# A two-layer hybrid decoder trunk on one core: the second half of layer 0's Q and K by token halves, with four query tiles of the first head between

## The chip, the cores and the metric

One core of a Trainium2 chip runs the whole program. The metric is the time of one execution in device microseconds. TensorE (PE) multiplies, VectorE (DVE), ScalarE (ACT) and GpSimd (POOL) do the rest, SyncE (SP) issues the transfers.

## The reference

Input and output are 1024 tokens x 1024 channels, float32. Layer 0 has differential attention (four heads, two 64-wide maps each) beside a pooling mixer, layer 1 a gated short convolution beside dilated attention with three branches; both end in an output projection and a SwiGLU block. What the change touches:

```python
q, k, v, u = jnp.split(proj, [qk_w, 2 * qk_w, 2 * qk_w + A_WIDTH], axis=-1)
q = rmsnorm(q.reshape(bsz, seq, 2, A_HEADS, HEAD_DIM), ev_q_gain[i])
k = rmsnorm(k.reshape(bsz, seq, 2, A_HEADS, HEAD_DIM), ev_k_gain[i])
...
s = jnp.einsum('bqmhd,bkmhd->bmhqk', qb, k, preferred_element_type=jnp.float32) * scale
s = s - slopes[:, None, None] * dist.astype(jnp.float32)
p = jax.nn.softmax(jnp.where(dist >= 0, s, -jnp.inf), axis=-1)
a = p[:, 0] - lam * p[:, 1]
o = jnp.einsum('bhqk,bkhd->bqhd', a.astype(v.dtype), v)
...
ya = (rmsnorm(ya, ev_subln_gain[i]) * (1.0 - lambda_init)).reshape(bsz, seq, A_WIDTH)
```

## The kernel before

**Split products.** Every float32 operand of a large product is split into a high part, made by ScalarE (`copy`, L1671), and a low part, the difference, made by VectorE (`low`, L2220) or GpSimd. A product is three matmuls of 512 columns (`mm3`, L1142 to L1144): high x high, low x high, high x low.

**Q and K.** The Q and K columns of layer 0 come in two halves `s`. A half runs over four quarters `q` of the channels; for each, SP loads raw weights (RQ, L661 on), ScalarE and VectorE split them into the buffers WQh and WQl (number r = 4s + q, two buffers by turns), and TensorE adds six matmuls to each of eight banks, one for each tile of 128 tokens. In the last quarter each bank ends with `qk_pe`. Then, for each token tile, ScalarE squares (SQ), VectorE sums (QSS, L2480) and scales (QMS, L2481), GpSimd raises to the power -1/2 (QRS, L1009, in a loop), VectorE applies it (QN, L2496), TensorE turns it by four transposes (`qk_turn`, L1352) and ScalarE writes it out (QK). In the first quarter of the second half TensorE also does two mixings (`mix`) of the pooling mixer.

**Attention of layer 0.** It runs over four heads, here units, of eight query tiles each, 32 tiles n. For a tile: scores of two maps (`score`, L1196 and L1197: keys K against queries QST, or K1X, K2X, QX in unit 0); bias and row extreme (`biased`, L2524: PR, NMX); exponential with its sum (`expo`, L1881); VectorE's reciprocal, ratio and combined tile (`combine`, L2578, semaphore `c_ok`); TensorE's transposes (`turn`, L1226); ScalarE's copy PT (`turned`); the product with V (`weigh`, L1238); ScalarE's squared sum and scaled copy (`scaled`, L1969: YJ, then Y). The order on every engine is written out by hand, and semaphores carry the rest. TensorE scores tile n+2, weighs n-1 and turns n. The stage begins when Q and K are all done.

**The keys of the next unit.** The keys and queries of unit u+1 are split while unit u runs: `next_stack` on ScalarE, `low_stacks` on GpSimd (K, L1019, and QST), each behind a combined tile (`behind_sum` waits for `c_ok`). When both K low parts exist, SP issues four transfers (L701, L702) that copy K with its halves of the partitions swapped (`staged`), and the first score of the next unit waits for all four. From tile n=7 on TensorE fills its time with blocks of the output projection (`out_block`, weights QWh and QWl, whose low part GpSimd makes at L1035).

**Layer 1** has the same loop over tiles with three branches; its ScalarE splits the next unit's keys in `following`, behind i=1 and i=2.

```python
def behind_sum(n):
    pool.wait_ge(c_ok, n + 1)
```

## Time and profile before

| | us |
|---|---|
| median of 3 runs | 2162.61 |
| fastest and slowest | 2161.91, 2162.73 |
| the profiled execution | 2162.4 |
| its span in the profile | 2160.5 |
| TensorE busy | 2126.2 (98%) |
| VectorE busy | 1306.7 (60%) |
| ScalarE busy | 900.1 (42%) |
| GpSimd busy | 862.0 (40%) |

The profiled execution's own time is 1.9 us longer than its span, which begins with the first and ends with the last instruction. The granted clock of TensorE is 0.9 or more of full speed in all 40 slices. In the views below a row gives the start, the duration, the engine, the line, the operation and the tiles; in brackets stand the idle time before it and what ended it.

### The profile page before, as it was taken

The page shows a single profiled execution, that of the slowest core. Times are in us where ns is not written, and L with a number is a line of the kernel's source. Part 1 is how long each engine was busy: PE and PEld are TensorE (multiplying, and loading weights), DVE is VectorE, ACT ScalarE, POOL GpSimd, SP SyncE. Part 2 cuts the span into 40 slices and gives each one's busy share as a digit, 9 for nine tenths or more (in the row PEclk, how much of TensorE's full clock was granted, in tenths as well). Part 3 has the DMA queues.
Part 4 walks back from the last instruction along what each step waited for, and adds up shares of the span by engine and source line. Part 5 has one row for each costly group of instructions (what it writes and reads, how often), then busy time and mean ns, then how long its engine had stood idle before and what let it go on. Part 6 is the DMA issues. An engine that isn't in the chain of part 4 may idle for free.

```text
span 2160.5 us, 30068 instructions
## 1 busy us (share of the span) xinstructions
PE 2126.2 (98%) x10572; PEld 1773.0 (82%) x10572; DVE 1306.7 (60%) x1725; ACT 900.1 (42%) x1497; POOL 862.0 (40%) x571
## 2 busy tenths in 40 slices
PE   8999899999999999999999999999999999999999
PEld 7877799888888888888888887888888888888887
DVE  4344775775565565558597347765865556555555
ACT  4134875443333333445333137853433333334432
POOL 1022432456677663002064024320577667751000
PEclk9999999999999999999999999999999999999999
DMA  5012321055554557676302120411265554558665
GB/s 193 0 52 56 127 79 30 20 168 202 187 185 164 175 175 261 198 244 194 117 20 59 59 69 21 135 44 38 69 205 190 198 174 153 169 176 283 194 194 195
DMA packets 229534, 295.55 MB, mean 137 GB/s; under 512 B 11824, under 2 KB 133168, under 8 KB 229168
## 3 DMA queue, kind: packets, MB, share of 16 engines
q1 hardware_dynamic: 229136, 294.04, 41.8%
q8 instruction: 68, 1.11, 0.2%
q14 instruction: 42, 0.34, 0.1%
q10 hardware_dynamic: 288, 0.05, 0.0%
HBM read 208.06 MB, written 77.59 MB: 132 GB/s over the span
## 4 chain that ended last, share of the span: by engine, by line
PE 80%; issue 13%; ACT 4%; POOL 2%; DVE 2%; DMA 1%; POOLq 0%; SPq 0%; ACTq 0%; DVEq 0%
PE PS L1613 12%; PE PS L1614 12%; PE PS L1615 12%; PE PS L1640 6%; PE PS L1642 6%; PE PS L1641 6%; PE PS L1142 4%; PE PS L1144 4%; PE PS L1143 4%; PE PS L1226 2%; PE PS L1265 1%; POOL QRS L1009 1%; ACT PR L1881 1%; PE PS L1331 1%; PE PS L1332 1%
## 5 line engine op out<-in xcount | busy, mean ns | idle before, releaser
L2220 DVE TENSOR_TENSOR LINEl<-LINE,HIGH 128x1024 fp32r<-128x1024 f32 x154 | 194.6, 1273 | 163.6 <-ACT HIGH L1671 163.5
L1671 ACT ACTIVATE HIGH<-LINE 128x1024 fp32r<-128x1024 f32 x154 | 162.7, 1060 | 232.2 <-PE PS L1642 208.2
L1640 PE MATMUL PS<-HIGH 128*128 128x512 f32 x616 | 240.2, 390 | 0.4 <-DVE LINEl L2220 0.4
L1642 PE MATMUL PS<-HIGH,LINEl 128*128 128x512 f32 x616 | 239.7, 389 | 0.0
L1641 PE MATMUL PS<-LINEl,HIGH 128*128 128x512 f32 x616 | 239.7, 389 | 0.0
L2220 DVE TENSOR_TENSOR SLOTl<-BLOCKS,RING 128x512 fp32r<-128x512 f32 x168 | 154.4, 919 | 95.6 <-ACT RING L1671 90.8
L941 POOL TENSOR_TENSOR ST<-ST 128x512 f32<-128x512 f32 x132 | 191.9, 1454 | 32.7 <-DMA ST<-in_ffn_w_down 24.1
L1671 ACT ACTIVATE RING<-BLOCKS 128x512 fp32r<-128x512 f32 x168 | 105.9, 630 | 227.8 <-PE PS L1615 221.5
L2220 DVE TENSOR_TENSOR SLOTl<-SLOT,RING 128x512 fp32r<-128x512 f32 x126 | 131.8, 1046 | 86.6 <-ACT RING L1671 86.3
L1009 POOL TENSOR_TENSOR QRS<-QMS,EXPO 128x8 f32<-128x8 f32 x32 | 52.1, 1638 | 220.7 <-DVE QMS L2481 220.1
L1640 PEld LDWEIGHTS PS<-HIGH 128*128 128x128 f32 x616 | 115.6, 188 | 24.9 <-DVE LINEl L2220 1.1
L1642 PEld LDWEIGHTS PS<-HIGH,LINEl 128*128 128x128 f32 x616 | 115.6, 188 | 24.0
L1641 PEld LDWEIGHTS PS<-LINEl,HIGH 128*128 128x128 f32 x616 | 115.7, 188 | 23.9
L1671 ACT ACTIVATE RING<-SLOT 128x512 fp32r<-128x512 f32 x126 | 79.2, 630 | 125.3 <-PE PS L1615 115.0
L1613 PE MATMUL PS<-B1h,RING 128*128 128x512 f32 x336 | 130.7, 389 | 0.0
L1614 PE MATMUL PS<-B1l,RING 128*128 128x512 f32 x336 | 130.7, 389 | 0.0
L1615 PE MATMUL PS<-B1h,SLOTl 128*128 128x512 f32 x336 | 130.7, 389 | 0.0
L913 POOL TENSOR_TENSOR SLOT<-BLOCKS 128x512 f32<-128x512 f32 x42 | 55.2, 1314 | 189.0 <-DMA BLOCKS<-in_ffn_w_up 189.0
L946 POOL TENSOR_TENSOR RST<-MSQ,EXPO 128x1 f32<-128x1 f32 x32 | 22.8, 714 | 224.3 <-DVE MSQ L2238 224.3
L1142 PE MATMUL PS<-WQh,HH 128*128 128x512 f32 x256 | 102.5, 400 | 0.6 <-DVE U L2533 0.6
L1144 PE MATMUL PS<-WQh,HL 128*128 128x512 f32 x256 | 99.9, 390 | 0.0
L1143 PE MATMUL PS<-WQl,HH 128*128 128x512 f32 x256 | 99.7, 389 | 0.0
(426 smaller groups left out, 5703.8 us busy)
## 6 DMA issues: line engine op xcount, KB each, us to landing
LINE<-hidden SPq DMA_DIRECT2D x154, 256.0 KB, 2.8
hidden<-HID SPq DMA_DIRECT2D x44, 512.0 KB, 4.3
ST<-in_ffn_w_down SPq DMA_DIRECT2D x44, 512.0 KB, 4.1
sums<-ST SPq DMA_DIRECT2D x22, 1024.0 KB, 6.1
hidden<-ST SPq DMA_DIRECT2D x22, 1024.0 KB, 6.7
LINE<-sums SPq DMA_DIRECT2D x88, 256.0 KB, 3.0
BLOCKS<-in_ffn_w_gate SPq DMA_DIRECT2D x42, 512.0 KB, 4.0
BLOCKS<-in_ffn_w_up SPq DMA_DIRECT2D x42, 512.0 KB, 5.2
```

Of the source, the lines that this page charges most:

```text
L941: nc.gpsimd.tensor_tensor(dst, x, y, op).then_inc(st_sum, 1)
L1142: pe.matmul(dst, lh, rh, start=first, stop=False)
L1143: pe.matmul(dst, lh, rl, start=False, stop=False)
L1144: return pe.matmul(dst, ll, rh, start=False, stop=last)
L1613: pe.matmul(dst, lh, rh[:, k, :], start=k == 0 and not adds_on, stop=False, skip_group_check=adds_on)
L1614: pe.matmul(dst, lh, rl[:, k, :], start=False, stop=False, skip_group_check=adds_on)
L1615: last = pe.matmul(dst, ll, rh[:, k, :], start=False, stop=k == 3, skip_group_check=adds_on)
L1640: pe.matmul(dst, hi[:, 0, ts], hi[:, 1, :], start=j == 0 and not adds_on, stop=False, skip_group_check=adds_on)
L1641: pe.matmul(dst, hi[:, 0, ts], lo[:, 1, :], start=False, stop=False, skip_group_check=adds_on)
L1642: pe.matmul(dst, lo[:, 0, ts], hi[:, 1, :], start=False, stop=j == NJ - 1, skip_group_check=adds_on).then_inc(dn_pe, 1)
L1671: return nc.scalar.activation(dst, src, ACT.Copy, **kw)
L2220: return v.tensor_tensor(dst, src, hi.bitcast(F32), ALU.subtract)
```

## The change

The second half of layer 0's Q and K is done by token halves: four quarters for token tiles 0 to 3, then four for tiles 4 to 7, in the order 2, 3, 1, 0, so that two of the weight buffers are kept and two (r=8, 9) are loaded and split again. Between the matmuls of the second token half stand the QK turns of tiles 0 to 3, the scores of tiles n=0 to 4 and the turns and weighings of n=0 to 3 of unit 0, with banks of their own (`score_at`, `turn_bank`, `weighed`) and outputs in a tile Y0. ScalarE's and VectorE's orders follow. The squared sum writes into the tile of the scaled copy, which now waits for it (`y_sq`). GpSimd's powers are unrolled; the low part of the first output weights is done in four rows of 256 columns between the last powers, and all low parts of unit 1's keys and first queries stand behind the combined tile n=4 (they stood behind n=2, 3 and 4). SP issues the tables before the loads of r=6 on, and the swap of unit 0 ahead of the output weights. In layer 1 ScalarE's high parts of the next keys stand behind i=0 and within i=1 (they stood behind i=1 and i=2), and two high parts of the convolution's columns move likewise in the last unit.

The core of the diff:

```diff
+        WQ_AT = (0, 10)
+        EARLY = 4
+        def score_at(L, m, n):
+            return 512 * m if L == 0 and n < EARLY else 1024 * m
+        def y_at(n):
+            return Y0[:, n, :] if n < EARLY else Y[:, n % NT, P * (n // NT):P * (n // NT) + P]
...
+                for r in range(6):
+                    load_qk(r, r // 4, r % 4)
+                if L == 0:
+                    load_tables()
+                    for r, q in ((6, 2), (7, 3), (8, 1), (9, 0)):
+                        load_qk(r, 1, q)
+                    swap_keys(0)
+                    sp.wait_ge(wq_lo, WQ_AT[1])
+                    load_quarter(0)
...
+                def low_quarter_row(k):
+                    if k == 0:
+                        pool.wait_ge(wo_hi, SPLIT_AT["q0"])
+                    ins = nc.gpsimd.tensor_tensor(QWl[0][:, k, :], QWs[0][:, k, :], QWh0[:, k, :].bitcast(F32), ALU.subtract)
+                    if k < 3:
+                        ins.then_inc(pool_part, 1)
+                        pool.wait_ge(pool_part, k + 1)
+                    else:
+                        ins.then_inc(wo_lo, 1)
+                        pool.wait_ge(wo_lo, SPLIT_AT["q0"])
...
-                    low_w("q0", QWl[0][:], QWs[0][:], QWh0[:])
-                    behind_sum(2)
-                    low_stacks(1, 0)
-                    behind_sum(3)
-                    low_stacks(1, 1)
-                    behind_sum(4)
-                    low_stacks(1, 2, 3)
+                    qk_power(2 * NT - 4)
+                    qk_power(2 * NT - 3)
+                    pool.wait_ge(qk_rs, 2 * NT - 2)
+                    low_quarter_row(0)
+                    qk_power(2 * NT - 2)
+                    pool.wait_ge(qk_rs, 2 * NT - 1)
+                    low_quarter_row(1)
+                    qk_power(2 * NT - 1)
+                    pool.wait_ge(qk_rs, 2 * NT)
+                    low_quarter_row(2)
+                    low_quarter_row(3)
+                    behind_sum(EARLY)
+                    low_stacks(1, 0, 1, 2, 3)
...
+                def qk_group(t, q, step):
+                    ts = slice(P * t, P * t + P)
+                    for r in range(2):
+                        last = mm3(bank(t), HH[:, 2 * q + r, ts], HL[:, 2 * q + r, ts], WQh[q % 2 if step < 6 else 1 - q % 2][:, r, :],
+                                   WQl[q % 2 if step < 6 else 1 - q % 2][:, r, :], step % 4 == 0 and r == 0, step % 4 == 3 and r == 1)
+                    if step % 4 == 3:
+                        last.then_inc(qk_pe, 1)
+                    elif step in (0, 1, 4, 5) and t % 4 == 3:
+                        last.then_inc(wq_pe[0], 1)
+                def qk_by_tokens():
+                    for step in range(4):
+                        pe.wait_ge(wq_lo, 4 + step + 1)
+                        for t in range(4):
+                            if step == 0:
+                                pe.wait_ge(bank_free[0], NT + t + 1)
+                                pe.wait_ge(mix_ok, 2)
+                            qk_group(t, step, step)
+                            if step == 0 and t < 2:
+                                mix(2 + t)
+                    pe.wait_ge(mix_ok, 4)
+                    for step, q in ((4, 2), (5, 3), (6, 1), (7, 0)):
+                        if step >= 6:
+                            pe.wait_ge(wq_lo, step + 3)
+                        for t in range(4, NT):
+                            if step == 4:
+                                pe.wait_ge(bank_free[0], NT + t + 1)
+                            qk_group(t, q, step)
+                            k = 4 * (step - 4) + t - 4
+                            if k < 4:
+                                qk_turn(1, k)
+                            if k == 3:
+                                pe.wait_ge(staged[0], 64)
+                                pe.wait_ge(stack_lo, 4)
+                                pe.wait_ge(bank_free[0], 2 * NT + 2)
+                                both_scores(0)
+                            elif k == 4:
+                                both_scores(1)
+                            elif k == 6:
+                                both_scores(2)
+                                turn(0, 0, 0, 0)
+                            elif k == 7:
+                                weigh(0)
+                            elif k == 8:
+                                both_scores(3)
+                                turn(0, 0, 0, 1)
+                            elif k == 9:
+                                weigh(1)
+                            elif k == 10:
+                                turn(0, 0, 0, 2)
+                            elif k == 11:
+                                weigh(2)
+                                turn(0, 0, 0, 3)
+                            elif k == 12:
+                                weigh(3)
+                                pe.wait_ge(s_mx[1][0], EARLY + 1)
+                                score(0, 0, 0, 0, EARLY)
+                            elif k == 14:
+                                pe.wait_ge(t_ea[0][0], EARLY)
+                                pe.wait_ge(o_ok[0], EARLY + 2)
+                                score(0, 1, 0, 0, EARLY)
+                    qk_turn(1, 4)
+                    qk_turn(1, 5)
+                    both_scores(5)
+                    qk_turn(1, 6)
+                    turn(0, 0, 0, EARLY)
+                    qk_turn(1, 7)
+                    both_scores(6)
...
+                def scaled(n):
+                    u, i = n // NT, n % NT
+                    c = 2 * (i % 4)
+                    act.wait_ge(o_pe[0], n + 1)
+                    nc.scalar.activation(y_at(n), weighed(n), ACT.Square, scale=RDN[:, c:c + 1],
+                                         accum_out=YSS[:, n:n + 1]).then_inc(y_sq, 1)
+                    act.wait_ge(y_sq, n + 1)
+                    copy(y_at(n), weighed(n), scale=RDN[:, c:c + 1]).then_inc(o_ok[0], 1)
...
-                    nc.scalar.activation(YJ[:], weighed(n), ACT.Square, scale=RDN[:, c:c + 1],
-                                         accum_out=YSS[:, n:n + 1]).then_inc(y_sq, 1)
-                    copy(Y[:, i, P * u:P * u + P], weighed(n), scale=RDN[:, c:c + 1]).then_inc(o_ok[0], 1)
...
+                    qk_square(1, 0)
+                    qk_square(1, 1)
+                    qk_square(1, 2)
+                    qk_out(1, 0)
+                    qk_square(1, 3)
+                    qk_out(1, 1)
+                    qk_out(1, 2)
+                    split_qk(0, 8)
+                    qk_out(1, 3)
+                    expos(0)
+                    expos(1)
+                    turned(0, 0, 0)
+                    expos(2)
+                    split_qk(0, 9)
+                    scaled(0)
+                    turned(0, 0, 1)
+                    expos(3)
+                    scaled(1)
+                    turned(0, 0, 2)
+                    scaled(2)
+                    turned(0, 0, 3)
+                    qk_square(1, 4)
+                    scaled(3)
+                    qk_square(1, 5)
+                    qk_square(1, 6)
+                    high_w("q0", QWh0[:], QWs[0][:])
+                    qk_out(1, 4)
+                    qk_square(1, 7)
+                    expos(EARLY)
+                    qk_out(1, 5)
+                    next_stack(0, 1, 1, 0, 1)
+                    qk_out(1, 6)
+                    expos(EARLY + 1)
+                    turned(0, 0, EARLY)
+                    qk_out(1, 7)
+                    next_stack(0, 1, 1, 2, 3)
+                    high_u(2, stacks_before(0, 1) + 2)
+                    for n in range(EARLY + 1, TILES0):
...
+                        if i == 1:
+                            following(1)
+                        if n == TILES0 - 7:
+                            channel_high(1)
                         turned(1, g, i)
                         if n + 1 < TILES0:
                             expo(1, g, i + 1)
-                        following(*{1: (0,), 2: (1,), 3: (2, 3), 4: (4,), 5: (5,)}.get(i, ()))
+                        following(*{0: (0,), 3: (2, 3), 4: (4,), 5: (5,)}.get(i, ()))
...
+                    qk_stats(1, 0)
+                    qk_stats(1, 1)
+                    qk_apply(1, 0)
+                    qk_stats(1, 2)
+                    qk_apply(1, 1)
+                    qk_stats(1, 3)
+                    qk_apply(1, 2)
+                    qk_apply(1, 3)
+                    biased(0, 0, 0, 0)
+                    biased(1, 0, 0, 0)
+                    split_qk(0, 8)
+                    for n in range(EARLY):
+                        if n + 1 < EARLY:
+                            if n > 0:
+                                dve.wait_ge(c_ok, n)
+                            biased(0, 0, 0, n + 1)
+                        for m in range(2):
+                            dve.wait_ge(s_ex[m][0], n + 1)
+                        denominators(n)
+                        if n + 1 < EARLY:
+                            biased(1, 0, 0, n + 1)
+                        ratio(n)
+                        combine(n)
+                        if n == 1:
+                            split_qk(0, 9)
+                    qk_stats(1, 4)
+                    dve.wait_ge(c_ok, EARLY)
+                    biased(0, 0, 0, EARLY)
+                    qk_stats(1, 5)
+                    qk_apply(1, 4)
+                    biased(1, 0, 0, EARLY)
+                    qk_stats(1, 6)
+                    qk_apply(1, 5)
+                    qk_stats(1, 7)
+                    qk_apply(1, 6)
+                    for n in range(EARLY, TILES0):
```

How the rows move, at three places. First TensorE, where the second half of Q and K ends and unit 0 begins (IDN is the identity of a transpose, QN a normalised QK tile, K1X and K2X the keys of unit 0 and their swapped copy, QX its queries). Before:

```order
L1352 MATMUL PS<-IDN,QN_102 128x128 [waits qk_n]
L1352 MATMUL PS<-IDN,QN_102 128x128 x3
L1196 MATMUL PS<-K1X_339,QX_343 128x256 [waits s_mxA0]
L1197 MATMUL PS<-K2X_341,QX_343 128x256
L1196 MATMUL PS<-K1X_340,QX_344 128x256 [waits s_mxB0]
L1197 MATMUL PS<-K2X_342,QX_344 128x256
L1352 MATMUL PS<-IDN,QN_103 128x128 [waits qk_n]
L1352 MATMUL PS<-IDN,QN_103 128x128 x3
L1196 MATMUL PS<-K1X_339,QX_343 128x384 [waits s_mxA0,stack_lo,mix_ok]
L1197 MATMUL PS<-K2X_341,QX_343 128x384
L1196 MATMUL PS<-K1X_340,QX_344 128x384 [waits s_mxB0]
L1197 MATMUL PS<-K2X_342,QX_344 128x384
```

And in the changed kernel, in the middle of the second token half, where PR are combined tiles and PT their turned copies:

```order
L1276 MATMUL PS<-IDN,PR_353 128x128 [waits c_ok,t_eaA0]
L1276 MATMUL PS<-IDN,PR_353 128x128 x2
L1189 MATMUL PS<-WQh_54,HH 128x512
L1190 MATMUL PS<-WQl_56,HH 128x512
L1191 MATMUL PS<-WQh_54,HL 128x512
L1189 MATMUL PS<-WQh_54,HH 128x512
L1190 MATMUL PS<-WQl_56,HH 128x512
L1191 MATMUL PS<-WQh_54,HL 128x512
L1288 MATMUL PS<-V,PT_349 128x128 [waits o_ok0,t_eaA0]
L1288 MATMUL PS<-V,PT_349 128x128 x2
L1276 MATMUL PS<-IDN,PR_354 128x128 [waits c_ok,t_eaA0]
L1276 MATMUL PS<-IDN,PR_354 128x128 x3
```

Turns and weighings of unit 0 stand between groups of QK matmuls, where before unit 0's scores came only behind the last of them.

Second, GpSimd from the last powers to UL. Before:

```order
L1009 TENSOR_TENSOR QRS<-QMS,EXPO 128x8 [waits qk_ms]
L1006 REGISTER_ALU
L1006 COMPARE_AND_BRANCH
L1035 TENSOR_TENSOR QWl_81<-QWs_77,QWh_85 128x1024 [waits wo_hi]
L1019 TENSOR_TENSOR K_333<-QK,K_333 64x1024 [waits stack_hi,stack_lo,c_ok,wo_lo]
L1019 TENSOR_TENSOR K_334<-QK,K_334 64x1024 [waits stack_hi,stack_lo,c_ok]
L1019 TENSOR_TENSOR QST_104<-QK,QST_104 64x256 [waits stack_hi,stack_lo,c_ok]
L1019 TENSOR_TENSOR QST_105<-QK,QST_105 64x256 [waits stack_lo,stack_hi]
L1030 TENSOR_TENSOR UL_70<-U,UH_66 128x1024 [waits uh_hi,c_ok,stack_lo]
```

In the changed kernel:

```order
L1048 TENSOR_TENSOR QWl_81<-QWs_77,QWh_85 128x256 [waits wo_hi,qk_rs]
L1035 TENSOR_TENSOR QRS<-QMS,EXPO 128x8 [waits qk_ms,pool_part]
L1048 TENSOR_TENSOR QWl_81<-QWs_77,QWh_85 128x256 [waits qk_rs]
L1035 TENSOR_TENSOR QRS<-QMS,EXPO 128x8 [waits qk_ms,pool_part]
L1048 TENSOR_TENSOR QWl_81<-QWs_77,QWh_85 128x256 [waits qk_rs]
L1048 TENSOR_TENSOR QWl_81<-QWs_77,QWh_85 128x256 [waits pool_part]
L1060 TENSOR_TENSOR K_333<-QK,K_333 64x1024 [waits stack_hi,stack_lo,c_ok,wo_lo]
L1060 TENSOR_TENSOR K_334<-QK,K_334 64x1024 [waits stack_lo,stack_hi]
L1060 TENSOR_TENSOR QST_104<-QK,QST_104 64x256 [waits stack_lo,stack_hi]
L1060 TENSOR_TENSOR QST_105<-QK,QST_105 64x256 [waits stack_lo,stack_hi]
L1071 TENSOR_TENSOR UL_70<-U,UH_66 128x1024 [waits uh_hi,c_ok,stack_lo]
```

QWl is made in four pieces, and the second K waits for no combined tile of its own; the first still does, for a later one.

Third, ScalarE in the second and third tile of a unit of layer 1. Before:

```order
L1671 ACTIVATE PT_350<-PS 128x128 [waits o_pe1,t_peB1]
L1881 ACTIVATE PR_354,DEN<-PR_354,NMX 128x256 [waits s_mxB1]
L1671 ACTIVATE PTB_355<-PS 128x256 [waits o_pe1,t_peA1]
L1881 ACTIVATE PR_351,DEN<-PR_351,NMX 128x384 [waits s_mxA1]
L1671 ACTIVATE PTB_356<-PS 128x256 [waits o_pe1,t_peB1]
L1881 ACTIVATE PR_353,DEN<-PR_353,NMX 128x384 [waits s_mxB1]
L1671 ACTIVATE K_333<-QK 64x1024
L1671 ACTIVATE PT_349<-PS 128x384 [waits o_pe1,t_peA1]
L1881 ACTIVATE PR_352,DEN<-PR_352,NMX 128x512 [waits s_mxA1]
L1671 ACTIVATE PT_350<-PS 128x384 [waits o_pe1,t_peB1]
L1881 ACTIVATE PR_354,DEN<-PR_354,NMX 128x512 [waits s_mxB1]
L1671 ACTIVATE K_334<-QK 64x1024
```

In the changed kernel:

```order
L1999 ACTIVATE PR_352,DEN<-PR_352,NMX 128x256 [waits s_mxA1]
L1789 ACTIVATE PT_350<-PS 128x128 [waits o_pe1,t_peB1]
L1999 ACTIVATE PR_354,DEN<-PR_354,NMX 128x256 [waits s_mxB1]
L1789 ACTIVATE K_333<-QK 64x1024
L1789 ACTIVATE PTB_355<-PS 128x256 [waits o_pe1,t_peA1]
L1999 ACTIVATE PR_351,DEN<-PR_351,NMX 128x384 [waits s_mxA1]
L1789 ACTIVATE K_334<-QK 64x1024
L1789 ACTIVATE PTB_356<-PS 128x256 [waits o_pe1,t_peB1]
L1999 ACTIVATE PR_353,DEN<-PR_353,NMX 128x384 [waits s_mxB1]
L1789 ACTIVATE PT_349<-PS 128x384 [waits o_pe1,t_peA1]
L1999 ACTIVATE PR_352,DEN<-PR_352,NMX 128x512 [waits s_mxA1]
```

Both K high parts now stand ahead of the exponential of 128x384 of the second map, and the first of them ahead of the first map's.

## Rows read from the trace of the kernel before

**Rows 1.** The page, busy time of TensorE.

```profile
PE 2126.2 (98%) x10572; PEld 1773.0 (82%) x10572; DVE 1306.7 (60%) x1725; ACT 900.1 (42%) x1497; POOL 862.0 (40%) x571
```

**Rows 2.** TensorE's waits, 212 to 246: waited for, us, times, longest.

```profile
PE PS L1238 <- ACT PT L1671: 4.9, 5, 1.7
PE PS L1352 <- DVE QN L2496: 1.6, 2, 1.1
PE PS L1196 <- DVE NMX L2524: 1.2, 3, 0.7
```

**Rows 3.** Timeline of TensorE around the first score of unit 1.

```profile
236.04 0.30 PE L1196 MATMUL PS<-K,QST 128*128 128x128 f32 x1
...
237.40 1.60 PE L1238 MATMUL PS<-V,PT 128*128 128x128 f32 x12 [0.94 <-ACT PT L1671]
...
242.07 1.83 PE L1238 MATMUL PS<-V,PT 128*128 128x128 f32 x14 [1.69 <-ACT PT L1671]
...
244.77 0.36 PE L1142 MATMUL PS<-QWh,UH 128*128 128x256 f32 x1
```

**Rows 4.** Timeline of TensorE in the second half of Q and K.

```profile
195.18 0.39 PE L1142 MATMUL PS<-WQh,HH 128*128 128x512 f32 x1
...
203.79 0.39 PE L1144 MATMUL PS<-WQh,HL 128*128 128x512 f32 x1
```

**Rows 5.** ScalarE's groups by form, 160 to 300: busy, mean ns, idle.

```profile
L1913 ACT ACTIVATE SQ<-PS 128x512 f32<-128x512 f32 x8 | 4.8, 597 | 15.6 <-PE PS L1144 15.6
```

**Rows 6.** VectorE's groups by form, 160 to 300.

```profile
L2496 DVE TENSOR_TENSOR QN<-PS,QRS 128x256 f32<-128x256 f32 x18 | 6.8, 420 | 1.4 <-POOL QRS L1009 1.2
...
L2480 DVE TENSOR_REDUCE QSS<-SQ 128x8 f32<-128x512 f32 x8 | 5.4, 680 | 11.0 <-ACT SQ L1913 11.0
...
L2220 DVE TENSOR_TENSOR WQl<-RQ,WQh 128x1024 fp32r<-128x1024 f32 x3 | 3.7, 1224 | 7.9 <-ACT WQh L1671 7.8
...
L2578 DVE SCALAR_TENSOR_TENSOR PR<-PR,SCB,PR 128x640 f32<-128x640 f32 x3 | 2.6, 880 | 0.0
...
L2524 DVE CUSTOM_DVE_ANT_0 PR<-PS,BX 128x768 f32<-128x768 f32 x2 | 1.9, 958 | 0.0
```

**Rows 7.** Timeline of GpSimd, 199 to 246.

```profile
201.74 13.29 POOL L1009 TENSOR_TENSOR QRS<-QMS,EXPO 128x8 f32<-128x8 f32 x8 [41.91 <-DVE QMS L2481]
215.00 2.39 POOL L1035 TENSOR_TENSOR QWl<-QWs,QWh 128x1024 fp32r<-128x1024 f32 x1
...
226.02 2.41 POOL L1019 TENSOR_TENSOR K<-QK,K 64x1024 fp32r<-64x1024 f32 x1 [0.69 <-DVE PR L2578]
```

**Rows 8.** Timeline of SyncE's issues, 228 to 231.

```profile
228.45 0.46 SPq L701 DMA_DIRECT2D K<-K  x1
...
230.25 1.12 SPq L702 DMA_DIRECT2D K<-K  x1
```

**Rows 9.** Issue to landing: transfers one and three (L701), then the fourth (L702).

```profile
DMA to landing us min/median/max: 3.0/3.7/4.4
...
DMA to landing us min/median/max: 4.8/4.8/4.8
```

**Rows 10.** Timeline of ScalarE, one scaled tile of unit 0.

```profile
221.98 0.19 ACT L1969 ACTIVATION_READ_ACCUMULATOR YJ<-PS,RDN 128x1 f32 x1
222.07 0.35 ACT L1671 ACTIVATE Y<-PS,RDN 128x128 f32<-128x128 f32 x1
```

**Rows 11.** TensorE's waits, 245 to 420.

```profile
PE PS L1238 <- ACT Y L1671: 0.8, 4, 0.3
```

**Rows 12.** Timeline of ScalarE in unit 1 of layer 1.

```profile
1349.32 1.06 ACT L1671 ACTIVATE K<-QK 64x1024 fp32r<-64x1024 f32 x1
```

**Rows 13.** Timeline of TensorE in the same unit.

```profile
1345.16 0.55 PE L1226 MATMUL PS<-IDN,PR 128*128 128x128 f32 x3
...
1352.00 0.77 PE L1226 MATMUL PS<-IDN,PR 128*128 128x128 f32 x5 [0.99 <-ACT PR L1881]
```

**Rows 14.** Timeline of VectorE, combined tile n=0.

```profile
216.79 0.74 DVE L2578 SCALAR_TENSOR_TENSOR PR<-PR,SCB,PR 128x128 f32<-128x128 f32 x1
```

358 lines of the change are left out of this document (193 added, 165 removed).

## The prediction

> **What bounds the kernel now.** I read the page first: TensorE is busy for 2126.2 of the span's 2160.5 us [rows 1], its granted clock is full in every slice, and the chain that ended last is four fifths TensorE's. The number of its matmuls does not change, so the time can only come out of its idle gaps. The profiled execution took 2162.4 us, 0.2 below the median of 2162.61; the sum goes against its span and carries over unchanged. A measurement tells about 0.2%, 4.3 us, from no change.
>
> The next view is TensorE's waits in the stretch the change rebuilds. Between 212 and 246 us it waits 7.7 us for three things: 4.9 for ScalarE's copy of the turned tile (PT), 1.6 for VectorE's normalised Q and K (QN) and 1.2 for VectorE's row extremes (NMX) [rows 2]. With a start-up of some tenths behind each of the ten, that is the most this part can win, 8 to 10 us. The reader should see that these gaps stand in two places, ahead of the first score of unit 1 (tile n=8, at 236.04) and behind it, 0.94 and 1.69 [rows 3]. From that score on TensorE's list of work is the same before and after, and what it has done up to it is the same too, in another order. So the question is when that score can start.
>
> **1. The earlier steps.** A step of the second half is 48 matmuls long now; from 195.18 to 203.79 there are 38 intervals, 0.2266 each [rows 4], so a step is 10.9 us and a half step 5.4. The half steps need split weights twice as often. For the fourth half step (r=7), buffer 1 is free when the second ends, about 176.6 (a start at 162.3, 10.9 for two half steps, 3.4 for the two mixings); ScalarE's high part takes 1.06, as the keys' of 1024 columns [rows 12], and VectorE's low part 1.22 [rows 6], so 178.9 if neither is busy and about 180.5 behind a UL and a hand-over. It is needed at 182.0. I cost it at nothing: the mixings and the third half step hide it. If that cover were gone, every us of lateness over 1.5 is one at the end. The two extra splits (r=8, 9) add 2.1 to ScalarE, 2.4 to VectorE and four loads to SP; their half steps come 11 us behind their buffers' release, so the four score and turn groups between them hide these, at nothing. In units of work ScalarE has room: eight squares at 0.60 [rows 5], the outputs, eight exponentials and four scaled tiles come to some 23 us of 31.
>
> **2. When the K swap of unit 1 can start.** SP issues it once GpSimd's two low parts of the keys are made. Before, the second ran from 226.02 for 2.41 [rows 7], the first of four transfers was issued at 228.45 and the last at 230.25 [rows 8], which took 4.8 to land [rows 9]: 6.6 from first issue to last landing, 235.0. The score came at 236.04 without a wait.
>
> After, both low parts stand behind the combined tile n=4. I follow that back. Tile 5's last matmul group ends at 162.3 + 30 groups x 1.36 + 3.4 for mixings + 1.8 for four turned QK tiles + about 6.8 for unit 0's pieces put in between = 215.1. Then its square 0.60, its sums 0.68 [rows 5, 6], a scaling of about 0.2, and GpSimd's power 1.66 (eight took 13.29 [rows 7]): 218.3. GpSimd now puts a quarter of the low part of the output weights, 2.39 for 1024 columns [rows 7] and so about 0.7 for 256, between powers, and the power for tile 6 ends at 220.8. VectorE applies it in 0.8 (two of 0.42), makes the row extremes of two tiles of 768 keys, 0.96 each, one small ratio and the combined 128x640 of 0.88 [rows 6]: 224.8. Two low parts make it 229.8, and the swap lands at 229.8 + 6.6 = 236.4. TensorE, which without any wait would be at that score near 228 (236.04, less 5.1 for the waits ahead of it, less about 0.3 of start-up behind each), waits for it. It waits on the way too, for QN of tiles 5 and 6 (about 1.4), for the combined tile n=4 (about 2.5) and for row extremes (about 1), and would be there at 233. None of that is summed: the swap, 3.5 us later, decides. **Term 1: +0.4 to +0.6, I take +0.5.** Bounds: if TensorE did not wait for the swap, 233 against 236.04, -3.0, and -3.5 with a shorter wait on the way; if the low parts ran 1 us later, +1.5.
>
> **3. Behind that score.** While TensorE waits, ScalarE and VectorE get ahead. Of 0.94 and 1.69 [rows 3] I leave 1.0 and 0.3. **Term 2: -1.3** (0 to -2.6). The first fill, at 244.77 before [rows 3], would come near 244.0.
>
> **4. The scaled tiles.** Square and scaled copy now write the same tile, so the copy waits for the square's accumulator. In the trace the copy starts at 222.07, 0.10 before the accumulator read ends (221.98 + 0.19) [rows 10]; with the wait it starts about 0.05 behind that end, so each tile costs ScalarE 0.15. The Trainium skill's page "ScalarE: Activation LUTs", section "What ACT_TABLE_LOAD costs", says that ACTIVATEs back to back overlap by about 93 ns; by that alone a tile would lose 0.09 and this term would be 0.7 instead of 1.2. The row's overlap of 0.10 agrees with it, and the hand-over is what I add. 24 tiles follow in units 1 to 3, 3.6 us in all, but TensorE waits for ScalarE's copy (Y) only in four of them, 0.8 us [rows 11]; the rest is hidden under the output blocks. I let a third reach the path. **Term 3: +1.2** (0 to +3.6).
>
> **5. Layer 1.** The keys' second high part, at 1349.32, delays the exponential behind it, for which TensorE's five turns wait 0.99 until 1352.00 [rows 12, 13]. Moved between the exponential of i=2 and the turned copy, and the first one an iteration earlier, 1.05 us now stands before the exponential for the three turns at 1345.16, which have no wait and no slack now [rows 13]. One wait of about 1.0 goes and one comes, in each of four units. **Term 4: +0.1** (-1 to +2). Late next, had the first high part been free, would be the QST copies.
>
> Sum: 0.5 - 1.3 + 1.2 + 0.1 = **+0.5 us, 2163.1**. The early work fills TensorE's gaps, but it then stands before the same swap.
>
> **The rivals.**
>
> *The gain is kept* (faster). The swap is not waited for so long, since GpSimd's low parts or the transfers end sooner. For it: the powers leave a loop and may be shorter, and the transfer share is low before the swap. Against it: each low part ran 2.39 and the four landings are spread by SP's own issue, 1.12 for the last [rows 8]. If the fourth transfer landed 3.0 after its issue, as the first did [rows 9], the swap took 4.8 and not 6.6; if the power and the low parts also came 1 us sooner, the score starts 2.8 earlier: 2160.3. In the bound, with no wait there at all, term 1 is -3.5 and the end 2159.1; with term 3 at nothing 2157.9. The page "DMA: Bandwidth & Descriptors" of the Trainium skill, section "Latency and other measured facts", gives about 600 ns to a first byte on such a queue; the row with 4.8 for a transfer of an undisturbed swap speaks against taking that as the whole price.
>
> *The turned copies are late at the early tiles* (slower). Four weighings now stand between QK groups, and TensorE's order is fixed: each waits for ScalarE's PT behind squares, splits and exponentials, as the five later ones do at 4.9/5 = 0.98 each [rows 2]. It decides from about 0.5 us of lateness, which is the room I find at them. Priced at 0.98 x 4 = 3.9, with the end of QK, and so the swap, later by that: 2163.1 + 3.9 = 2167.0. For it: VectorE may be held up beside GpSimd, since a combined tile of 128 keys took 0.74 while GpSimd's QWl ran, against 0.88 for 640 keys [rows 6, 14]. Against it: ScalarE's 23 of 31 us, and GpSimd is idle through the early tiles.
>
> *The moves do nothing*: gaps only change places in both layers, the self-wait is hidden: 2162.6. This and my forecast cannot be told apart by the time alone.
>
> **How the numbers follow.** The forecast with the nothing case: 0.76. The gain kept: 0.16, of which 0.08 goes beyond 4.3 us (under 2158.3). Turned copies late: 0.08, of which 0.06 beyond. Faster 0.09, same 0.84, slower 0.07. The range takes in the faster rival's middle and, above, the ends of terms 1 and 3 together: 2159.0 to 2166.0.
>
> **What would show it.** In the changed trace: no wait of TensorE between 163 and 218; waits at the fifth and sixth QK turns, then a longer one for the combined tile n=4 near 225; the wait for unit 1's keys of about 4 us ending near 236.5, and the swap's first issue near 229.9; fill near 244; more waits for Y in the main loop than 0.8; in layer 1 waits of about 1.0 at the three turns, none at the five. It is wrong if that wait for the keys is under 2 us, if waits stand among the QK groups, or if the layer 1 waits do not mirror each other.

## The result and the profile after

| | before | changed |
|---|---|---|
| median of 20 runs each, same chip | 2162.70 | 2165.97 |
| fastest and slowest | 2161.91, 2164.38 | 2163.90, 2169.03 |
| the profiled execution | 2162.4 | 2165.93 |
| its span | 2160.5 | 2164.1 |

The ratio is 1.0015, 95% interval 1.0008 to 1.0021: 3.3 us longer, inside the 0.2% (4.3 us) that the prediction calls no change, but with an interval that leaves 1 out. The forecast was 2163.1 with a range of 2159.0 to 2166.0, so the median lies inside the range, at its upper edge. The sum said +0.5 and the measurement says +3.3; most of what follows is about that difference.

The page of the changed kernel: its span, busy times, granted clock and chain (compare [rows 1]).

```profile
span 2164.1 us, 29989 instructions
...
PE 2128.2 (98%) x10572; PEld 1776.2 (82%) x10572; DVE 1302.6 (60%) x1728; ACT 906.2 (42%) x1499; POOL 871.3 (40%) x574
...
PEclk9999999999999999999999999999999999999999
...
PE 92%; ACT 3%; DVE 2%; POOL 1%; issue 1%; DMA 1%; SPq 0%; ACTq 0%; DVEq 0%; POOLq 0%
```

The page hides what matters here: TensorE is busy for 2.0 us more than before with the same work, and the row of clocks still shows only nines. TensorE's waits of the changed kernel from 160 to 246 us (waited for, us, times, longest), the counterpart of [rows 2]:

```profile
PE PS L1276 <- issue: 2.5, 1, 2.5
PE PS L1244 <- DMA K<-K: 2.2, 1, 2.2
PE PS L1244 <- DVE NMX L2693: 1.3, 2, 0.8
PE PS L1402 <- DVE QN L2665: 1.0, 1, 1.0
PE PS L1288 <- ACT PT L1789: 0.8, 1, 0.8
PE PS L1189 <- DVE U L2755: 0.6, 1, 0.6
```

The 4.9 us for PT have become 0.8. In their place stand 2.5 ahead of the turn of the combined tile n=4 (listed as "issue"; VectorE's combination of that tile ends at 225.32 and the turn starts at 225.41) and 2.2 for unit 1's keys. The last row is the one at 162, from which the rebuilt stretch begins; between it and 218 there is none. TensorE's timeline around the two standing waits, and to the first fill (L1189):

```profile
225.41 1.30 PE L1276 MATMUL PS<-IDN,PR 128*128 128x128 f32 x5 [2.53 <-issue]
...
237.49 0.33 PE L1244 MATMUL PS<-K,QST 128*128 128x128 f32 x1 [2.22 <-DMA K<-K]
...
237.76 2.33 PE L1288 MATMUL PS<-V,PT 128*128 128x128 f32 x12
...
242.92 1.83 PE L1288 MATMUL PS<-V,PT 128*128 128x128 f32 x14 [0.78 <-ACT PT L1789]
...
245.62 0.36 PE L1189 MATMUL PS<-QWh,UH 128*128 128x256 f32 x1
```

The first score of unit 1 starts 1.45 later than before and the fill, at 245.62, is 0.85 later than the 244.77 of [rows 3]. The wait for keys was there, and one wait of 0.78 in place of 0.94 and 1.69. But the 12 weighings at 237.76 took 2.33, where before they took 1.60 [rows 3]. What GpSimd, SyncE and VectorE did ahead of the swap (one fence for each):

```profile
223.90 2.00 POOL L1048 TENSOR_TENSOR QWl<-QWs,QWh 128x256 fp32r<-128x256 f32 x2
225.98 4.90 POOL L1060 TENSOR_TENSOR K<-QK,K 64x1024 fp32r<-64x1024 f32 x2
```

```profile
230.90 0.46 SPq L699 DMA_DIRECT2D K<-K  x1
...
232.69 1.12 SPq L700 DMA_DIRECT2D K<-K  x1
```

```profile
224.21 1.11 DVE L2712 SCALAR_TENSOR_TENSOR PR<-PR,SCB,PR 128x640 f32<-128x640 f32 x1
...
229.86 2.10 DVE L2677 SCALAR_TENSOR_TENSOR BIAS<-DIST,SM,MASK 128x1024 f32<-128x1024 f32 x1
```

The combined tile ends at 225.32, the low parts at 230.88, the swap is issued at 230.90 and TensorE goes on 6.59 later: the chain that the prediction followed, each link 0.5 to 1.0 late. GpSimd's last two rows of output weights, at 223.90, end only at 225.90 and then the keys begin.

The granted clock of TensorE shows where its longer busy time comes from. Stretches of the changed kernel (PE busy, PEld, DVE, ACT, POOL, then the granted clock, DMA share and GB/s):

```profile
222.00:224.00 2.00, 0.88 (x7) 0.47 (x5) 2.00 (x7) 1.98 (x6) 1.84 (x3) 1.00 0.00 0
224.00:225.00 1.00, 0.00 (x0) 0.00 (x0) 0.96 (x2) 0.97 (x2) 0.92 (x2) 0.84 0.00 0
225.00:228.00 3.00, 2.59 (x11) 2.52 (x12) 0.98 (x3) 3.00 (x7) 2.92 (x2) 0.50 0.00 0
...
236.00:238.00 2.00, 0.51 (x4) 0.51 (x5) 1.97 (x4) 1.97 (x7) 0.77 (x1) 1.00 0.38 59
238.00:239.00 1.00, 1.00 (x8) 1.00 (x8) 0.42 (x3) 1.00 (x2) 0.74 (x1) 0.67 0.73 238
239.00:241.00 2.00, 2.00 (x12) 2.00 (x11) 0.17 (x1) 0.96 (x3) 1.07 (x1) 0.50 1.04 406
241.00:242.00 1.00, 1.00 (x7) 0.94 (x5) 0.00 (x0) 0.05 (x1) 0.00 (x0) 0.62 0.76 274
```

Twice, once behind each standing wait, the granted clock is 0.50: 1.2 GHz of the 2.4. The first time its cost is swallowed by the wait for the keys. The second time little is waited for (0.8 for PT), and everything up to the fill pays. A third fall lies at the very start: the mean clock from 10 to 20 us is 0.83 in this profile and in those of kernels 1, 3, 4, 7, 9 and 10 below, and 1.00 in the others and before. Here it cost nothing that can be seen, since the rebuilt stretch begins at 162.16, and at 162.33 before.

Behind the fill, TensorE's waits for the scaled tiles from 245 to 420 us, against 0.8 in four [rows 11]; its waits for the exponentials in layer 1 from 1300 to 1440, where before had 5.6 us in nine with a longest of 1.2; and its timeline there, at the three turns that had no wait in [rows 13]:

```profile
PE PS L1288 <- ACT Y L1789: 2.4, 8, 0.5
```

```profile
PE PS L1276 <- ACT PR L1999: 5.4, 9, 0.9
```

```profile
1348.71 0.55 PE L1276 MATMUL PS<-IDN,PR 128*128 128x128 f32 x3 [0.90 <-ACT PR L1999]
```

The account of the profiled execution by these rows: +0.85 at the fill, +1.6 in the waits for Y, and +3.6 in the span, so about 1.1 is left. It stands in layer 1, in three small waits of TensorE: 1.3 for X where before had 0.5, 2.2 for QN where before had 1.9, and 0.5 for PTB where before had 0.2, less the 0.2 that the exponentials gave back.

```profile
PE PS L1189 <- DVE X L2578: 1.3, 1, 1.3
```

### The profile page after: what moved, and what is told of

It reads as the page before. It is cut to its first block, busy times and chain, and to the rows that moved or that the text cites. A ratio compares the mean times of both kernels' runs of the same rounds, so it can differ in the third digit from the quotient of the medians.

```text
span 2164.1 us, 29989 instructions
## 1 busy us (share of the span) xinstructions
PE 2128.2 (98%) x10572; PEld 1776.2 (82%) x10572; DVE 1302.6 (60%) x1728; ACT 906.2 (42%) x1499; POOL 871.3 (40%) x574
## 3 DMA queue, kind: packets, MB, share of 16 engines
q8 instruction: 68, 1.11, 0.2%
## 4 chain that ended last, share of the span: by engine, by line
PE 92%; ACT 3%; DVE 2%; POOL 1%; issue 1%; DMA 1%; SPq 0%; ACTq 0%; DVEq 0%; POOLq 0%
PE PS L1733 12%; PE PS L1731 12%; PE PS L1732 12%; PE PS L1189 7%; PE PS L1191 7%; PE PS L1190 7%; PE PS L1758 6%; PE PS L1760 6%; PE PS L1759 6%; PE PS L1276 2%; PE PS L1315 2%; PE PS L1381 1%; PE PS L1380 1%; PE PS L1382 1%; PE PS L1288 1%; PE PS L1207 1%
## 5 line engine op out<-in xcount | busy, mean ns | idle before, releaser
L972 POOL TENSOR_TENSOR RST<-MSQ,EXPO 128x1 f32<-128x1 f32 x32 | 22.8, 714 | 224.8 <-DVE MSQ L2407 224.8
L1189 PE MATMUL PS<-WQh,HH 128*128 128x512 f32 x256 | 103.2, 403 | 0.6 <-DVE U L2755 0.6
```

Source lines behind the costliest of these rows:

```text
L1189: pe.matmul(dst, lh, rh, start=first, stop=False)
```

## The experiments

Three sets of four kernels ran, each set on one chip beside the kernel before (33 runs of it a set, 11 of each other kernel). The interval of a ratio is about 2 us to either side throughout, so a profile's rows carry more than a median does. The profiles do not all reach the rebuilt stretch at the same time: its first matmul starts between 162.00 and 163.15 us (162.33 before, 162.16 and 162.09 in the changed kernel, 163.08 in kernel 4), and starts of different profiles differ by that before anything else. Medians are given as a difference to the kernel before in the same set.

| kernel | difference, us | ratio, 95% interval |
|---|---|---|
| the changed kernel, again | +3.6 | 1.0017 (1.0008, 1.0026) |
| 1: layer 0 only | +2.6 | 1.0009 (0.9999, 1.0018) |
| 2: no self-wait | +0.9 | 1.0003 (0.9994, 1.0012) |
| 3: keys early | +0.4 | 1.0003 (0.9994, 1.0012) |
| 4: matmuls in the gaps | +1.9 | 1.0008 (0.9999, 1.0017) |
| 5: three edits | -1.3 | 0.9994 (0.9985, 1.0003) |
| 6: three edits, gap filled | -1.5 | 0.9994 (0.9985, 1.0003) |
| 7: three edits, combine first | -1.7 | 0.9992 (0.9983, 1.0001) |
| 8: before with the self-wait | +2.8 | 1.0013 (1.0004, 1.0022) |
| 9: before with layer 1's edit | +0.6 | 1.0000 (0.9991, 1.0009) |
| 10: 7 with the weight rows behind the powers | -1.4 | 0.9993 (0.9984, 1.0002) |
| 11: 10 with the gap filled | -0.9 | 0.9996 (0.9987, 1.0005) |

(The ratio is taken over the set's rounds, so it need not be the quotient of the medians.)

### The changed kernel again

No edit. The question is what an execution without the second fall of the clock costs.

> The changed kernel once more, unedited, beside the others of this set. Expected: 2.5 to 3.5 us over the kernel before; in its profile the same waits as before (2.5, 2.2, Y 2.4), and the granted clock between 220 and 250 us at or under 1.0, differing from the first profile where the fall is a matter of the moment, the same where it is fixed by the waits.

Its profiled execution took 2163.61 (span 2161.8), against 2165.93. TensorE's timeline of it, the same matmuls as above:

```profile
237.45 0.33 PE L1244 MATMUL PS<-K,QST 128*128 128x128 f32 x1 [2.21 <-DMA K<-K]
...
237.72 1.55 PE L1288 MATMUL PS<-V,PT 128*128 128x128 f32 x12
...
241.25 1.83 PE L1288 MATMUL PS<-V,PT 128*128 128x128 f32 x14 [0.77 <-ACT PT L1789]
...
243.94 0.36 PE L1189 MATMUL PS<-QWh,UH 128*128 128x256 f32 x1
```

and two of its stretches:

```profile
225.00:228.00 3.00, 2.62 (x13) 2.34 (x14) 0.94 (x3) 3.00 (x7) 2.92 (x2) 0.69 0.00 0
...
239.00:241.00 2.00, 1.48 (x14) 1.27 (x12) 0.74 (x5) 1.66 (x4) 1.04 (x1) 1.00 0.97 375
```

One program, one list of waits, and the score of unit 1 within 0.04 us in both. Here the clock stayed full behind the wait for keys, the weighings took 1.55 instead of 2.33, and the fill came at 243.94 instead of 245.62. From score to fill it is 6.49 against 8.13: **the fall costs 1.64 us** there. It also shows what the forecast was a forecast of: without the fall the fill is at 243.94, where it said 244.0, and the span is 1.3 above before's.

The 31 runs of this kernel in both sets say the same: the 8 with a mean clock of 0.999 took 2163.6 to 2165.2 (median 2164.3), the 4 with 0.996 took 2168.1 to 2169.0. The kernel before has 33 runs with 0.999 on record, and their median is 2163.2. So at a like clock the two kernels are 1.0 apart, near the 1.3 of the two spans; the changed kernel's other 23 runs, all under 0.999, have a median of 2166.5.

### 1: layer 0 only

Layer 1's ScalarE order is put back, the two convolution columns too.

```diff
-                        if i == 1:
-                            following(1)
-                        if n == TILES0 - 7:
-                            channel_high(1)
...
-                        following(*{0: (0,), 3: (2, 3), 4: (4,), 5: (5,)}.get(i, ()))
+                        following(*{1: (0,), 2: (1,), 3: (2, 3), 4: (4,), 5: (5,)}.get(i, ()))
```

> The change in layer 0 alone; layer 1's high parts stand where they stood before. Theory (layer 1 costs little, the loss is in layer 0's clock and waits): the wait at the five turns of layer 1 is back at about 1.0 a unit and the one at the three turns is gone, the granted clock of TensorE still falls between 224 and 242 us, and the median is 0.4 to 1.0 us under the full change, about 2165.2. Rival (layer 1's new waits are the loss): the median falls back to before's, about 2162.7.

+2.6 in place of +3.3 and +3.6, far inside the interval. The waits for the exponentials in layer 1 are 5.7 with a longest of 1.2, as before the change. So layer 1 has no part in the result that could be told.

### 2: no self-wait

From the fifth tile on the square writes into the place of the next tile's output, which nothing has read or filled yet, and the copy waits only for the square of the tile before.

```diff
-                    nc.scalar.activation(y_at(n), weighed(n), ACT.Square, scale=RDN[:, c:c + 1],
+                    own = n < EARLY or n == TILES0 - 1
+                    nc.scalar.activation(y_at(n if own else n + 1), weighed(n), ACT.Square, scale=RDN[:, c:c + 1],
                                          accum_out=YSS[:, n:n + 1]).then_inc(y_sq, 1)
-                    act.wait_ge(y_sq, n + 1)
+                    act.wait_ge(y_sq, n + 1 if own else n)
```

> The full change, but from tile 4 on the squared sum writes its unused output into the place of the next tile, so that the scaled copy does not wait for it. Theory (the self-wait costs 0.15 us a tile on ScalarE and 1.5 us of TensorE's waits for Y): those waits, 2.4 us between 245 and 420, fall to about 0.8, and the median to about 2164.5. Rival (the self-wait is hidden, the waits for Y come from the changed phase of the engines): they stay near 2.4 and the median near 2166.

The waits for Y are back at 0.8 in four, and the difference to the kernel before is 2.4 smaller than the changed kernel's +3.3. The profiled execution was the longest of its kernel's 11, 2167.72, with the clock at 0.50 from 240 to 246: from score (237.53) to fill (248.09) it took 10.56, 4.1 more than the 6.49 above. A fall can cost more than the 1.6.

### 3: keys early

ScalarE's high parts of unit 1's keys are put behind the first scaled tile and the third turned copy, and GpSimd's low parts of them ahead of the last four powers, where it is idle.

```diff
                     scaled(0)
+                    next_stack(0, 1, 1, 0)
                     turned(0, 0, 1)
...
                     turned(0, 0, 2)
+                    next_stack(0, 1, 1, 1)
...
+                    low_stacks(1, 0)
+                    low_stacks(1, 1)
                     qk_power(2 * NT - 4)
...
-                    low_stacks(1, 0, 1, 2, 3)
+                    low_stacks(1, 2, 3)
```

> The full change, but unit 1's keys are split as soon as the fifth half step has freed their place: ScalarE's high parts behind the scaled tile 0 and the turned copy 2, GpSimd's low parts before its last four powers. Theory (the score of tile n=8 waits for the swap): its wait of 2.2 us is gone, the swap is issued before 214, TensorE comes to that score near 235.3; the second fall of the clock, 238 to 242, goes or shrinks; of the 2.2 + 1.5 us about 1 comes back as waits for PT; median 2163 to 2163.6. Rival (TensorE stands elsewhere just as long, and the clock falls anyway): within 0.5 us of the full change, 2165.5 to 2166.5.

TensorE's timeline in the profile of this kernel, the first score of unit 1 and the next weighings:

```profile
234.08 0.30 PE L1246 MATMUL PS<-K,QST 128*128 128x128 f32 x1 [0.42 <-DVE NMX L2696]
...
239.39 1.83 PE L1290 MATMUL PS<-V,PT 128*128 128x128 f32 x14 [1.54 <-ACT PT L1791]
```

The keys' low parts ran at 205.44 and 210.65, 2.4 each, and held nothing up. The wait for the transfer is gone, the score starts 1.96 sooner than before the change, and the span is 2160.2, 0.3 below before's even with the self-wait in place. The median, at +0.4, does not show that much. Of the 3.4 us by which the score came sooner than in the changed kernel, 0.8 went into a longer wait for PT (1.54 against 0.78). The gap of 2.5 ahead of the combined tile is still there, and here the clock stayed at 1.00 behind it; kernel 5 below shows what it costs when it does not.

### 4: matmuls in the gaps

Matmuls whose result nobody reads are put into the two standing waits: 11 of 512 columns ahead of the turn of tile n=4, and 9 ahead of the first score of unit 1, behind that score's wait for row extremes (which must hold before bank 0 is written).

```diff
                     qk_turn(1, 6)
+                    pe.wait_ge(bank_free[0], 2 * NT + 5)
+                    for _k in range(11):
+                        pe.matmul(bank(4), QX[0][:, 0:P], K1X[0][:, 0:HALF], start=True, stop=True)
                     turn(0, 0, 0, EARLY)
...
+                                for _k in range(9):
+                                    pe.matmul(bank(0), K1[1][0][:, 0:P], K1[1][0][:, 0:HALF], start=True, stop=True)
```

> The full change, with 11 matmuls of 512 columns that nobody reads before TensorE's wait for the combined tile n=4 and 9 before its wait for unit 1's keys; both waits stand about 2.5 and 2.2 us, so these matmuls lengthen nothing. Theory (TensorE's standing still there lowers its granted clock to half for some 3 us twice, and the second time is on the path): the granted clock between 220 and 250 us stays at 1.0, the fill starts 1.3 to 1.6 us earlier, the median is about 2164.5 with less spread. Rival (the clock falls by chance or for other reasons, or its fall is hidden): the clock in 220 to 250 stays near 0.9 and the median at 2166 or above.

Stretches of 10 us of this kernel's profile:

```profile
220.00:230.00 10.00, 8.51 (x47) 6.63 (x46) 7.78 (x19) 9.76 (x21) 9.29 (x8) 1.00 0.00 1
230.00:240.00 10.00, 7.89 (x36) 6.18 (x35) 9.08 (x13) 7.74 (x15) 6.79 (x5) 0.83 0.52 119
```

The filled gap left the clock at full speed. At 234.05 TensorE waited 1.98 for row extremes; VectorE's timeline of this kernel shows what made them late:

```profile
229.62 3.30 DVE L2685 SCALAR_TENSOR_TENSOR BIAS<-DIST,SM,MASK 128x1024 f32<-128x1024 f32 x1
...
232.92 1.06 DVE L2701 CUSTOM_DVE_ANT_0 PR<-PS,BX 128x896 f32<-128x896 f32 x1
```

The bias table, 2.10 in the changed kernel and 1.28 in the kernel before, took 3.30 (see the last section). My matmuls stood behind that wait and left this gap open, and behind it the clock fell. The 9 matmuls then ran into that fall:

```profile
236.56 3.43 PE L1582 MATMUL PS<-K 128*128 128x512 f32 x9
```

The swap of the keys was issued at 231.87, which with its 6.6 us puts the last landing near 238.5, and the score behind the 9 matmuls started at 239.83. So some 1.3 us of matmuls that nobody reads stood on the path here, where none were meant to, and the kernel's +1.9 can't be read as the changed kernel without its falls. It is half an experiment: a filled gap kept the clock in this execution, an unfilled one of 2 us lost it.

### 5 to 7: three edits together

5 is edits 1, 2 and 3 in one kernel. 6 adds the 11 matmuls of edit 4. 7 is 5 with VectorE's combination of tile n=4 ahead of the row extremes of tile 5, which shortens the gap itself:

```diff
+                        if n == EARLY:
...
+                            combine(i)
+                            dve.wait_ge(c_ok, n)
+                            biased(0, b, g, i + 1)
+                            biased(1, b, g, i + 1)
+                            qk_apply(1, 7)
+                            continue
```

> The full change with the keys of unit 1 split early, without the self-wait from tile 4 on, and with layer 1 as before: three costs taken away together. Theory (the costs are separate, so their parts add): against the full change -2.2 for the keys, -1.4 for the self-wait, -0.4 for layer 1, about 1.5 to 2 us under the kernel before, unless the clock falls in the gap before the combined tile n=4, which stays 2.5 us. Rival (what is freed is waited for by TensorE somewhere else): level with before.

> As the run n5_three, with 11 unread matmuls in TensorE's wait for the combined tile n=4. Theory (standing still lowers the clock): no fall of the granted clock between 220 and 250 us in the profile, and the runs scatter less and lie 0.5 to 1 us under n5_three on average. Rival (the fall is not tied to the gap): the fall shows here too as often, and the median equals that of n5_three or lies above it.

> As the run n5_three, with VectorE's combined tile n=4 ahead of the two row extremes of tile 5. Theory (TensorE's 2.5 us before the turn of tile 4 are a wait for that combined tile, which stands behind the extremes on VectorE): that gap shrinks to about 1 us, tile 5's exponentials start about 1 us later, which costs 0.3 to 0.5 at the weighings; in sum 0.5 to 1 us under n5_three and 2 to 3 us under before. Rival (the gap is set by the power of the fourth of these tiles on GpSimd): the gap stays over 2 us and the median at that of n5_three.

The three edits together bring the kernel to -1.3 us against the kernel before, where 1.5 to 2 was expected, and 1.3 to 1.7 is all that the token halves bring: the interval still takes in 1. Filling the gap (6) moved the median by 0.1, which is nothing; the profile of 6 has the clock at 1.00 from 220 to 260 and its span is 2159.1, the profile of 5 has 0.86 from 218 to 230 and 2160.3. With the keys early, a fall behind the first gap is no longer hidden: from the turn of tile n=4 to unit 1's first score kernel 5 took 9.96 us (225.50 to 235.46), kernel 3 8.26 (225.82 to 234.08) and kernel 6 8.25 (225.76 to 234.01). In 7 the gap shrank to 0.90, but behind the next turn stood a new wait. TensorE's waits of kernel 7, 212 to 246:

```profile
PE PS L1404 <- DVE QN L2663: 2.6, 2, 1.6
PE PS L1290 <- ACT PT L1791: 1.4, 1, 1.4
PE PS L1278 <- issue: 0.9, 1, 0.9
```

1.6 of the 2.5 moved from the combined tile to the last QK turn, and the clock fell here too: once behind that turn, and once more behind the wait of 1.4 for PT, after which the 14 weighings at 241.02 took 2.97, against 1.83 in kernel 5 behind the same wait. The expected 2 to 3 us under before became 1.7.

### 8 and 9: one part of the change alone in the kernel before

```diff
-                    act.wait_ge(o_ok[0], n + 2)
-                    nc.scalar.activation(YJ[:], weighed(n), ACT.Square, scale=RDN[:, c:c + 1],
+                    nc.scalar.activation(Y[:, i, P * u:P * u + P], weighed(n), ACT.Square, scale=RDN[:, c:c + 1],
                                          accum_out=YSS[:, n:n + 1]).then_inc(y_sq, 1)
+                    act.wait_ge(y_sq, n + 1)
```

> The kernel before, with one edit: the squared sum writes into the place of the scaled copy, which waits for it, and the wait for the copy before it goes. Theory (the self-wait costs the same in the old order): the scaled copy starts 0.47 to 0.50 behind the square in place of 0.34, TensorE's waits for Y between 245 and 420 rise from 0.8 to 2 or more, and the median by 1 to 1.5 us. Rival (hidden): nothing measurable, under 0.4 us.

This edit by itself made the kernel before slower by 2.8 us, with an interval clear of 1, about twice the 1 to 1.5 expected. ScalarE's timeline in it, one scaled tile:

```profile
242.58 0.37 ACT L1968 ACTIVATE Y<-PS,RDN 128x128 f32<-128x128 f32 x1
242.85 0.19 ACT L1968 ACTIVATION_READ_ACCUMULATOR Y<-PS,RDN 128x1 f32 x1
243.07 0.37 ACT L1671 ACTIVATE Y<-PS,RDN 128x128 f32<-128x128 f32 x1
```

The copy starts 0.49 behind the square; without the wait the same tile had 0.36 (242.04 and 242.40). So one tile costs 0.13. The Trainium skill's page "ScalarE: Activation LUTs", section "What ACT_TABLE_LOAD costs", says that ACTIVATEs back to back overlap by about 93 ns. The loss of that overlap alone would be 0.09 us a tile; the trace has 0.13, overlap and wait together, and the measurement decides. TensorE's waits in it, 212 to 246 and 245 to 420:

```profile
PE PS L1238 <- ACT PT L1671: 5.8, 5, 2.0
```

```profile
PE PS L1238 <- ACT Y L1671: 2.4, 8, 0.5
```

0.9 more for PT and 1.6 more for Y make 2.5. The profile's span, 2164.6, is 4.1 above before's, and the other 1.6 is the clock, which fell behind the longest of these waits for PT:

```profile
242.61 2.52 PE L1238 MATMUL PS<-V,PT 128*128 128x128 f32 x14 [1.97 <-ACT PT L1671]
...
246.91 0.39 PE L1142 MATMUL PS<-QWh,UH 128*128 128x256 f32 x1
```

From these weighings to the fill it is 4.30, where before had 2.70 [rows 3].

Kernel 9 is the kernel before with layer 1's edit as the changed kernel has it.

> The kernel before with the change's edit in layer 1 alone. Theory (one wait takes another's place): the waits for the exponential in layer 1 are 5.4 in place of 5.6 us, all at the three turns and none at the five, and the median lies 0 to 0.7 us over before. Rival (the high parts moved forward pay): over 1 us under before.

+0.6, not told from nothing. Its waits for the exponentials mirror as predicted, 5.4 with a longest of 0.9. It also had the clock at 0.86 from 218 to 230: such falls are not the changed kernel's alone. There the wait for PT was 3.6 and not 4.9, so the slower clock was hidden in it. And it fell behind no long wait: the longest between 212 and 220 is 1.1, the one just before the fall 0.7.

### 10 and 11: the rows of output weights out of the way

All four rows of 256 columns go behind the last power, to let the powers and so the last QK turns come sooner; 11 adds 5 unread matmuls in the gap of 10.

```diff
-                    pool.wait_ge(qk_rs, 2 * NT - 2)
-                    low_quarter_row(0)
                     qk_power(2 * NT - 2)
-                    pool.wait_ge(qk_rs, 2 * NT - 1)
-                    low_quarter_row(1)
                     qk_power(2 * NT - 1)
                     pool.wait_ge(qk_rs, 2 * NT)
+                    low_quarter_row(0)
+                    low_quarter_row(1)
```

> As the run n7_three_combine, with the four pieces of the output weights' low part behind the last power in place of between them. Theory (the pieces delay the last two powers by 0.7 and 1.4 us, and so the QK turns of the last tiles): TensorE's 2.6 us of waits for QN fall to about 1.5, the median to 0.5 to 1 us under n7_three_combine, 2.2 to 2.7 under before. Rival (VectorE's combined tile now meets a piece and waits for it, or the turn is not what the rest waits for): as n7_three_combine.

> As the run r3_rows_after, with 5 unread matmuls ahead of the turn of tile n=4. Theory (TensorE standing still there is what lowers its clock): the granted clock stays at 1.0 between 220 and 250 us, and the slowest runs come nearer to the fastest; median 0 to 0.5 us under r3_rows_after. Rival: the matmuls are 1.1 us of work on the path, and the median rises by up to that.

A miss: 1.4 under before, where 2.2 to 2.7 was expected. The waits for QN stayed at 2.6. VectorE's timeline in kernel 10 says why:

```profile
223.59 0.95 DVE L2689 CUSTOM_DVE_ANT_0 PR<-PS,BX 128x768 f32<-128x768 f32 x1
...
224.47 0.95 DVE L2689 CUSTOM_DVE_ANT_0 PR<-PS,BX 128x768 f32<-128x768 f32 x1
...
225.34 0.75 DVE L2661 TENSOR_TENSOR QN<-PS,QRS 128x256 f32<-128x256 f32 x2
```

The last power ended at 223.23, but VectorE puts its result to use at 225.34, behind two rows of extremes. It was VectorE's order and not GpSimd's rows that held the turn. Kernel 11's profiled execution has the clock at 1.00 up to 260 and the shortest span of all, 2158.9; its median is none the better for it, 0.5 over kernel 10's, where 0 to 0.5 under was expected.

## Why the prediction came out as it did

**Right: the frame.** TensorE bounds the kernel, its matmuls are the same, and the gaps changed places. No wait stands among the QK groups from 163 to 218, so step 1, the split weights and the four early weighings at nothing, held, and so fell the rival with turned copies late. The gap ahead of the combined tile was put at 2.5 and is 2.5, ending at 225.4 for "near 225". The wait for the keys was put at about 4, with anything under 2 as a sign of being wrong; it is 2.2.

**Right in kind, off by one: term 1.** Low parts done at 230.88 for 229.8, swap issued at 230.90 for 229.9, score at 237.49 for 236.4: +1.45 for +0.5. The swap's own 6.6 was exact (6.59). The us was lost ahead of the low parts: the combined tile ended at 225.32 instead of 224.8, and GpSimd's last two rows of output weights, 1.00 each where I had 0.7, ended only at 225.90, behind it. TensorE came to the wait at 235.3, not 233, so the wait was 2.2 and not 4; that is free, and it means that only about two of the three us in my lower bound could be had. Kernel 3 had 1.96. Of the two QK turns that were to wait only the fifth did, 1.0 instead of 1.4.

**Right in kind, too small: term 2.** 0.78 is left of 0.94 and 1.69, where I left 1.3, and the whole stretch from score to fill shrank by 2.2 (8.73 before, 6.49 undisturbed) instead of 1.3. Terms 1 and 2 made -0.8 together, and the undisturbed fill, at 243.94, is -0.83. That agreement is luck: one term was 0.9 too low, the other 0.9 too high.

**Mis-sized: term 3.** One tile costs 0.13, close to the 0.15 that was said. I let a third of 24 tiles reach the path "since TensorE waits for ScalarE's copy only in four of them". That was the step that was mis-sized. A wait that is absent in a profile can be absent by less than the 0.13 that is added. With 0.13 more on each, eight tiles waited instead of four, for 1.6 more, and the same delay went through the turned copies in the place where they were already late: 2.5 by the waits and 2.8 by the medians (kernel 8), two thirds and more of its upper bound of 3.6. In the changed kernel the part at PT is hidden by the wait for keys, and what shows is the 1.6.

**Missing: the granted clock.** The prediction read that the clock was full in every slice and took it for given. Of 7.8 us of waits in this stretch the change gathers 4.7 into two, of 2.5 and 2.2, and behind these the clock fell to half. Behind the first this is hidden, as long as the keys are waited for; behind the second it costs 1.64, in the executions in which it happens. The term has no row in the trace of before, which was taken in an execution with a full clock throughout; still, a forecast that puts a standing wait of 2.5 and one of 4 on TensorE should have asked what it costs to start again. It belongs in the range's upper end. That the median stayed inside the range, by 0.03 us, is luck: nothing in the sum stood for the clock, and the same kernel's 11 runs in the later set have a median of 2166.52, above the range.

**Right: term 4.** Waits of 0.90 at the three turns, none at the five; +0.1 was said; kernel 9 against the kernel before gives +0.6, the changed kernel against kernel 1 +0.7 (3.3 and 2.6), neither told from zero.

By these, the changed kernel in an execution without the second fall is -0.83 at the fill, +1.6 for Y and some 0.5 behind it, which are layer 1's waits for X, QN and PTB (0.7, 2.2 and 0.5, against 0.5, 1.9 and 0.2): +1.3, against +0.5. These three waits had no term; why they grew was not tested. The median's +3.3 holds 2.0 more. The fall behind the keys gives 1.6 of it where it happens, and up to 4.1 was seen. That the rest are further falls is likely by the runs' mean clocks (23 of 31 under 0.999), but no edit showed it: adding matmuls to the gaps took away the slowest runs (kernel 4 lies between 2164.46 and 2166.27, the changed kernel between 2163.61 and 2169.03) and did not take the median back to +1.3, and kernel 4 pays for its own matmuls.

The rival "the gain is kept" had its mechanism right in kernel 3: with the keys out of the way the score starts 1.96 sooner, in an execution in which the clock stayed up. Even then, with the self-wait taken out too, only 1.3 to 1.7 of it arrive at the end.
